# Gathering V apart from U in five of eight slots, with rows of weight zero left out

## The reference, cut to what matters

```
q = (xt @ w_query).reshape(TOKEN_BLOCK, PEER_HEADS, 2, PEER_HALF)
s = einsum('thpd,hpnd->thpn', q, sub_keys)
s_top, i_top = lax.top_k(s, 16)
...
best, pos = lax.top_k(cand, 16)          # 16 experts for each token and each of 8 heads
idx = take_along_axis(cand_idx, pos)
g = softmax(best)
u = expert_u[idx]
v = expert_v[idx]
act = gelu(einsum('td,thkd->thk', xt, u))
return einsum('thk,thkd->td', g * act, v)
```

## Time and profile before

| | us |
|---|---|
| median of 3 runs (1540.13 to 1544.98) | 1541.23 |
| the profiled execution's own time | 1543.3 |
| its span in the trace | 1541.5 |

### The profile page before, as it was taken

How to read it: one execution, slowest core, us unless ns; L and a number is a source line. 1 busy time by engine, 2 the same in 40 slices (tenths; PEclk the granted TensorE clock), 3 DMA queues, 4 the chain that set the end, 5 groups by cost and what they waited for, 6 DMA issues and landing times.

```text
span 1541.5 us, 24488 instructions
## 1 busy us (share of the span) xinstructions
PE 1415.1 (92%) x8308; PEld 1060.6 (69%) x8308; DVE 1099.3 (71%) x2390; ACT 785.9 (51%) x1804; POOL 342.2 (22%) x445
## 2 busy tenths in 40 slices
PE   9999999999999999999999899999877887777877
PEld 8898999998889999998989864444222332222222
DVE  6667877777768777577897687666666667666644
ACT  6656544456665444476964435444444444444433
POOL 1010011110110111111110134333333333333331
PEclk9999999999999999999999999999999999999999
DMA  9999899999999999999999499999999999999996
GB/s 356 355 337 334 281 399 398 388 392 340 353 325 331 403 389 403 386 362 337 344 329 352 149 388 414 422 421 421 421 422 421 421 420 422 422 421 421 417 422 266
DMA packets 119268, 578.23 MB, mean 375 GB/s; under 512 B 11472, under 2 KB 11616, under 8 KB 85904
## 3 DMA queue, kind: packets, MB, share of 16 engines
q0 software_dynamic: 79584, 432.01, 72.3%
q1 hardware_dynamic: 39168, 142.97, 24.6%
q10 hardware_dynamic: 432, 2.19, 0.4%
HBM read 576.08 MB, written 135.27 MB: 461 GB/s over the span
## 4 chain that ended last, share of the span: by engine, by line
PE 60%; DMA 23%; DVE 9%; ACT 5%; issue 3%; POOL 0%; POOLq 0%; DVEq 0%; ACTq 0%
DMA attn<-expert_uv,idx 15%; PE PS L655 8%; PE PS L651 8%; PE PS L646 8%; PE PS L1179 8%; PE PS L1143 7%; DMA ada<-w_ada 4%; DMA late<-expert_uv,idx 3%; PE PS L779 3%; PE PS L677 2%; PE PS L1106 2%; PE PS L889 2%; PE PS L893 2%; PE PS L894 2%; ACT wrg L1591 2%
## 5 line engine op out<-in xcount | busy, mean ns | idle before, releaser
L2360 DVE CUSTOM_DVE_ANT_0 late<-late,PS 128x1024 f32<-128x1024 f32 x128 | 156.2, 1220 | 112.9 <-DMA late<-expert_uv,idx 112.9
L1666 DVE TENSOR_TENSOR early_splits<-ring,early_splits 128x1024 fp32r<-128x1024 f32 x166 | 202.0, 1221 | 48.1 <-ACT early_splits L1245 47.9
L2360 DVE CUSTOM_DVE_ANT_0 attn<-attn,PS 128x1024 f32<-128x1024 f32 x128 | 156.1, 1220 | 96.7 <-DMA attn<-expert_uv,idx 95.0
L1245 ACT ACTIVATE early_splits<-ring 128x1024 fp32r<-128x1024 f32 x166 | 174.8, 1054 | 44.5 <-PE PS L646 35.7
L1583 ACT ACTIVATE gel<-dot 128x1 f32<-128x1 f32 x256 | 51.2, 200 | 266.9 <-DVE dot L2360 266.7
L1179 PE MATMUL PS<-late,wrg 128*128 128x512 f32 x288 | 145.3, 630 | 43.4 <-ACT wrg L1591 43.4
L593 POOL DMA_INDIRECT attn<-expert_uv,idx x128 | 120.9, 944 | 240.4 <-PE PS L1179 103.0
L1179 PE MATMUL PS<-attn,wrg 128*128 128x512 f32 x288 | 142.4, 619 | 31.8 <-ACT wrg L1591 31.6
L593 POOL DMA_INDIRECT late<-expert_uv,idx x128 | 119.9, 937 | 231.9 <-PE PS L1179 117.0
L1179 PEld LDWEIGHTS PS<-late,wrg 128*128 128x128 f32 x288 | 49.9, 191 | 135.4 <-ACT wrg L1591 98.1
L1179 PEld LDWEIGHTS PS<-attn,wrg 128*128 128x128 f32 x288 | 50.7, 193 | 123.5 <-ACT wrg L1591 82.3
(11 more groups left out here) (416 smaller groups left out, 3033.8 us busy)
## 6 DMA issues: line engine op xcount, KB each, us to landing
ring<-wstream SPq DMA_DIRECT2D x258, 512.0 KB, 9.1
expert_uv<-expert_u POOLq DMA_DIRECT2D x64, 1024.0 KB, 14.3
expert_uv<-expert_v POOLq DMA_DIRECT2D x64, 1024.0 KB, 15.8
ada<-w_ada POOLq DMA_DIRECT2D x32, 512.0 KB, 10.4
late<-w_ada POOLq DMA_DIRECT2D x16, 512.0 KB, 14.6
late<-wstream SPq DMA_DIRECT2D x4, 512.0 KB, 9.3
attn<-expert_uv,idx POOLq DMA_INDIRECT x128, 15.2
late<-expert_uv,idx POOLq DMA_INDIRECT x128, 15.2
```

The source lines that it names most:

```text
L1245: act.activation(hi_of(u), raw(u), ACT.Copy).then_inc(hi_ready, 1)
L1666: ve.tensor_tensor(lo_of(u), raw(u), hi_of(u).bitcast(F32), ALU.subtract).then_inc(units_begun, 1)
L2360: ve.tensor_tensor_reduce(row, row, H2N[n // 8], 1.0, 0.0, ALU.mult, ALU.add, dot[:, n % 2, k:k + 1]).then_inc(dot_ready, 1)
```

## The change

Slots 1, 4 and 7 (`JOINT`) stay as they were. In the other five slots POOL gathers only U from `expert_u` (4 KB a token), and V later, from `expert_v`, with a gather of its own, four rows later in POOL's list (`V_LAG`). Before that V gather DVE makes its indices (`pick_row`): the row's index where the weight is not zero, and that index plus 2^20 where the weight equals zero. The gather has a bound, and an index above it is passed over, so that nothing is copied for that token; what lay in the buffer stays and is multiplied by zero. U may be gathered again into a separate slot as soon as the dot of the row before in that slot is done (`dot_ready`); V waits for `row_used`. PE waits for `v_landed`, which is `row_landed` in the joint slots.

```diff
+JOINT = (1, 4, 7)
+V_LAG = 4
+NO_ROW = float(1 << 20)
...
+        idx_v = sb("idx_v", [P, SLOTS], U32)
+        no_row = sb("no_row", [P, SLOTS])
...
+        v_landed = [row_landed[k] if k in JOINT else sem(f"v_landed{k}") for k in range(SLOTS)]
+        tokens_marked, rows_picked = sem("tokens_marked"), sem("rows_picked")
...
+        def separate(rows):
+
+            return rows // SLOTS * (SLOTS - len(JOINT)) + sum(k not in JOINT for k in range(rows % SLOTS))
...
+                s = i % SLOTS
+                at = bass.IndirectOffsetOnAxis(ap=idx[:, n % 3, k:k + 1], axis=0)
+                if s in JOINT:
+                    if i >= SLOTS:
+                        gp.wait_ge(row_used, i - SLOTS + 1)
+                    gp.indirect_dma_start(UV[s], None, expert_uv, at).then_inc(row_landed[s], 16)
+                else:
+                    if i >= SLOTS:
+                        gp.wait_ge(dot_ready, i - SLOTS + 1)
+                    gp.indirect_dma_start(UV[s][:, 0:D], None, expert_u, at).then_inc(row_landed[s], 16)
+
+            def row_v(i):
+
+                s = i % SLOTS
+                if s in JOINT:
+                    return
+                gp.wait_ge(rows_picked, separate(i + 1))
                 if i >= SLOTS:
                     gp.wait_ge(row_used, i - SLOTS + 1)
-                gp.indirect_dma_start(UV[i % SLOTS], None, expert_uv,
-                                      bass.IndirectOffsetOnAxis(ap=idx[:, n % 3, k:k + 1], axis=0)
-                                      ).then_inc(row_landed[i % SLOTS], 16)
-
-            for i in range(ROWS):
-                row(i)
+                gp.indirect_dma_start(UV[s][:, D:2 * D], None, expert_v,
+                                      bass.IndirectOffsetOnAxis(ap=idx_v[:, s:s + 1], axis=0),
+                                      bounds_check=NKEYS * NKEYS - 1, oob_is_err=False).then_inc(v_landed[s], 16)
+
+            for i in range(ROWS + V_LAG):
+                if i < ROWS:
+                    row(i)
+                if i >= V_LAG:
+                    row_v(i - V_LAG)
...
             def weigh(i):
-                pe.wait_ge(row_landed[i % SLOTS], 16 * (i // SLOTS + 1))
+                pe.wait_ge(v_landed[i % SLOTS], 16 * (i // SLOTS + 1))
...
+            def pick_row(i):
+
+                n, k, s = i // EXPK, i % EXPK, i % SLOTS
+                if s in JOINT:
+                    return
+                ve.wait_ge(w_ready, i + 1)
+                ve.tensor_scalar(no_row[:, s:s + 1], wts[:, s:s + 1], 0.0, NO_ROW, ALU.is_equal,
+                                 ALU.mult).then_inc(tokens_marked, 1)
+                if i >= SLOTS:
+                    ve.wait_ge(v_landed[s], 16 * (i // SLOTS))
+                ve.wait_ge(tokens_marked, separate(i + 1))
+                ve.tensor_tensor(idx_v[:, s:s + 1], no_row[:, s:s + 1], idx[:, n % 3, k:k + 1],
+                                 ALU.add).then_inc(rows_picked, 1)
...
                     row_dot(n * EXPK + k)
+                    if n or k:
+                        pick_row(n * EXPK + k - 1)
```

More of the change, by code:

```diff
@@ L1175, in weigh_rows @@
                     for m in range(SLOTS):
-                        pe.wait_ge(row_landed[m], turn * 16 + 16 * (first // SLOTS + 1))
+                        pe.wait_ge(v_landed[m], turn * 16 + 16 * (first // SLOTS + 1))
                         pe.wait_ge(diag_ready, turn * SLOTS + (first + m + 1))
```

## The result

The changed kernel takes 1726.37 us (median of 4 runs, 1717.78 to 1731.4) against 1542.33 (4 runs) beside it: ratio 1.1184, interval 1.1156 to 1.1212. The forecast was 1574, range 1518 to 1620. The direction was right; the size was not, by 152 us. What follows reads the two profiled executions.

A forecast was written before the change was run, and what follows sets the result against it. The prediction took the DMA engines (99% busy, 420 to 422 GB/s) to bound the lookup. Its terms, +21 + 39 + 8 + 9 - 52 + 8 = +33 us on the median of 1541.2, gave 1574, range 1518 to 1620.

The forecast's parts named there:

- the dear gather: Rival: each bounded gather costs POOL 0.66 us more, 2.43 us a row, total 1623 us; chance 12%.
- the rival of zeros not skipped: Rival: zero-weight V rows are fetched in effect, steady rows at 2.49 or above, the gain goes, 1626 us; chance 8%.
- short flights: Rival: with engines running, a flight's fixed 3.0 us is smaller by 1.4, -24 over some 17 flights, 1550 us; chance 10%.
- -52: Gain in the steady rows: rows 72 to 127 16 us, rows 144 to 255 36 us, together -52.
- I take 2.20: Pace assumed for the steady rows, in us a row, between 2.13 by bytes and 2.27 by the loop.
- Half-size packets cost nothing by themselves: Bytes step: 4 KB packets keep 421 GB/s, as the weight stream in slices 1 to 23 was read to show.
- The loop that I did compute, 2.27 a row: Steady rows: dot, pick, V issue, 5.5 us flight and V bytes ahead close a four-row loop in 9.1 us.
- 52.0 a head: Early heads 3 to 7: loops of 14.3, 8.3 and 29.4 us make a head 52.0 us instead of 38.9.
- 39 + 8: Early rows' loss: three whole heads (row 18 to 66) +39 us, the last head up to its scores +8.
- PE's clock, +8 (bounds 0 and 24): PE idles 3 to 5 us some 15 times; half of them at 1.6 us are 12, some hidden, taken as +8.
- the start (+21: Rows before row 18: scores +12, ten rows to row 18 +5, ScalarE's table switches +4, together +21 us.
- head 8 (+9: Head 8's first block, rows 128 to 143: three loops of 8.1 us, 24 us for 6 rows instead of 15, +9.

The follow-up runs named there:

- Run 3: The changed kernel with ScalarE taking PE's results four rows behind (gates three) instead of one, scores behind k = 10 instead of 8: 1609.07 us, ratio 1.041.
- run 6: Control: the kernel before the change with only the late takes of Run 3: 1539.59 us, ratio 0.9988.
- run 2: The changed kernel with the marker at 0 instead of 2^20, so every V row is read while picks, waits and bound stay: 1771.11 us, ratio 1.1458.
- run 13: As 12, but V right behind U in POOL's list and indices made seven rows ahead: 1521.24 us, ratio 0.9854.
- 12: As Run 3, but V rows left out by their index, made ahead of the dot; computes another sum, so no candidate: 1566.52 us, ratio 1.0171.
- run 7: As Run 3, but with the pick behind the row's own dot instead of the next row's: 1592.57 us, ratio 1.0323.
- run 9: The kernel before with five of eight slots gathered as separate U and V, V right behind U, nothing skipped: 1570.88 us, ratio 1.0172.
- 11: As run 7, but a V row is left out when its dot is under -6, so no weight is waited for: 1571.02 us, ratio 1.0184.
- Run 14: As 12 (V four rows later, indices made ahead), but no V row left out: 1595.19 us, ratio 1.0345.
- run 1: The changed kernel with V gathered by the row's own unbounded index, no pick or wait for it, every row read: 1594.9 us, ratio 1.0318.

## Why the prediction was right or wrong

**Right: the sign and its place.** The heads where ScalarE takes queries and scores lose most, by the loop that the prediction drew: takes, weight, pick, V issue, V flight, PE. Run 3 takes it apart and run 6 shows that nothing else hangs on the takes. The waits stand where they were forecast: VectorE waits 58.0 us for a weight between 900 and 1060 us, where "some tens" were said; ScalarE's takes wait longer than forecast, 9 to 16 us each in rows 16 to 79, for 6 to 9. Bytes fell by 36.8 MB (432.0 to 395.2 in the software queue; 38 forecast), which is 44% of the separate V rows, in the bounds of 41 to 50. The bounded gather takes 0.997 us to issue, forecast 0.94, in its bounds; the dear gather falls, and so does the rival of zeros not skipped (run 2: 41 us). V's flight in the loop shown, from the start of its issue to PE's start, is 1073.04 - 1069.26 = 3.8 us and V(0)'s 4.2, forecast 4.1. The rule of 2.0 us and bytes over 436 (the Trainium skill, "DMA: Bandwidth & Descriptors", section "Anatomy of one DMA") gives an estimate of 2.7 and does not hold here; "short flights" falls with it.

**Wrong: the term "-52", the steady rows.** Of it -13 were for rows 80 to 127 and -36 for rows 144 to 255 (the rest, rows 72 to 79, is counted with the early rows here). They lost 9.9 and 19.1: +29 where -49 stood. "I take 2.20" was 2.69. This one step is 78 us of the 152. The runs split the late pace: 2.13 by bytes at 421 GB/s; 2.36 when nothing waits, since the rate of full engines falls to 379 (run 13); 2.54 with the lag (12); 2.69 with the wait for the weight (7). The step that failed first is to take 421 GB/s over to the new packets. "Half-size packets cost nothing by themselves" is off by little (414 GB/s in run 9); most of the fall comes once rows are left out. Nor could carry the sentence: slices 1 to 23 show at most 403 GB/s, not 420, and a weight stream is no gather with rows left out. The loop that I did compute, 2.27 a row, took the 5.5 us flight of a lone gather for a joint row; in runs 11 and 12 joint rows fly 7.5 and 7.6 us (medians between 1250 and 1490 us). But run 7, whose loop spans five rows, keeps 2.69, so this loop alone does not set the pace.

**Wrong: the length of the loops, "52.0 a head".** Measured between takes: 16 us for 14.3, 11.4 for 8.3, 34.7 to 37.4 for 29.4, some 64 in all. Three differences are seen: the pick's end to POOL's issue takes 0.79 us where I had counted none beyond the pick; PE's row and its scores run at the lower clock, 3.78 and 1.91; and if the eight rows between go at 2.7, as elsewhere, in place of 2.20, that is 4 us a head. Rows 16 to 79 cost +95 where +45 stood (39 + 8, less 2 for rows 72 to 79).

**Wrong: "PE's clock, +8 (bounds 0 and 24)".** The idle times were seen, but the price was put on half of 15 rows. Each head has three such loops, and the granted clock goes down and up between its two levels through all of them: 0.54 in the window of 1072 to 1076 us, in which the row shown takes 3.78 us, and 1.00 in that of 1064 to 1068. The means are 0.83 and 0.85 between 940 and 1060 us, and 0.97 and 0.94 there once the takes are late (run 3). How many of the 95 us are the clock's own is not separated by these runs; in the loop shown it is 1.9 + 0.9 of 11.4. A bound, as an estimate: a mean of 0.83 over the 255 us of rows 16 to 79 is some 87 us at the lower level, so the halved speed itself can have cost at most 44 us there.

**Too low: the start (+21, measured +32) and head 8 (+9, measured +25).** V(0) goes out 2.3 us later than forecast: row 0's weight is done 1.6 us later than in the trace before, and POOL's issue starts 0.80 us after the pick. The early query, which POOL's row 7 waits for, starts behind PE's slow row 0:

```profile
895.33 1.00 POOL L622 DMA_INDIRECT attn<-expert_v,idx_v  x1 [7.14 <-DVE idx_v L2406]
...
899.50 3.78 PE L1175 MATMUL PS<-attn,wrg 128*128 128x512 f32 x4 [4.40 <-DMA attn<-expert_v,idx_v]
...
903.07 4.64 PE L1151 MATMUL PS<-soft,late 128*128 128x258 f32 x16
...
907.98 0.94 POOL L608 DMA_INDIRECT late<-expert_uv,idx  x1 [7.86 <-PE PS L1151]
```

POOL stands for 7.9 us there, with V(3) and the gathers of rows 8 and 9 behind it, and row 7 goes out at 907.98, before at 898.95. That wait (`freed_by_query`) was in the code, and I did not follow POOL past it. Head 8's six takes follow one another with no free rows between, so their 4.09 a row is that of the early heads. And the end was in no term: from the last dot's start to the end it is 15.3 us now, 8.7 before, since the last V is gathered behind its dot.

On the traces the error is 188 - 33 = 155 us, and these terms add up to it: 78 for the steady rows, 50 for rows 16 to 79, 16 for head 8, 11 for the start, 8 ahead of the first dot and at the end, less the 8 for the clock, whose price the measured stretches hold already. The direction was not luck: the loops cost what they were said to, and more. But the forecast held a gain of 52 us that does not exist here.

**Which rival was nearest.** None. Those above the forecast, 1623 and 1626, had other mechanisms, and both fell. What was missing is a case in which the gain itself does not come: engines that are not full any more because V is late, and that move less when they are.

## What to carry to other kernels

Where a kernel is bound by full DMA queues, bytes saved count in full only if the queues stay full and the rate stays the same: price the rate of the new packets, and what the new order of issues makes later, before the bytes. A load whose index hangs on the newest result turns every stall of the engines that make the result into an idle queue; count all in-order waits in that circle, those of unrelated work (here taking a query out of PSUM) first. An experiment that gives nearly the same bytes without the dependence (runs 12 and 13) tells early whether the idea has room: here 24 us at best, and none with the lag.

## What the runs showed of the hardware

Between 1300 and 1500 us (for the change 1430 to 1630, so that head 8's loops are not in it) the single packets' records in the traces give, at full or nearly full engines:

| kernel | GB/s, share | 8 KB packets, mean (median) ns | 4 KB, mean (median) ns | 4 B packets |
|---|---|---|---|---|
| before | 421, 1.01 | 314 (312) | | 1279 |
| halves, all rows (9) | 414, 1.02 | 315 (314) | 163 (161) | 2045 |
| halves, all rows, lag 4 (14) | 404, 1.01 | 325 (309) | 163 (159) | 2001 |
| halves, rows left out (13) | 379, 0.99 | 347 (309) | 165 (159) | 5489 |
| the change | 336, 0.93 | 354 (309) | 180 (159) | 4578 |

```profile
1430.00:1630.00 200.00, 150.24 (x297) 59.37 (x295) 137.00 (x419) 81.36 (x242) 116.68 (x122) 0.91 0.93 336
```

- A 4 KB packet takes 163 ns, 6 more than half of 314. That is the small price of halves in the late rows (run 9).
- A row left out still has a packet, but a cheap one: 4 bytes in place of 4 KB, 9 ns by the mean. The software queue has 102624 packets in run 1 and in the change alike; every gather also has 16 packets of 4 bytes of its own (1279 for 80 gathers in the kernel before). The counts show it:

```profile
DMA packets 18005, 80.81 MB, mean 404 GB/s; under 512 B 2001, under 2 KB 2001, under 8 KB 14284
```

```profile
DMA packets 18423, 70.49 MB, mean 352 GB/s; under 512 B 5053, under 2 KB 5053, under 8 KB 14591
```

(Run 14, then 12.) The 3052 more of them at 9 ns are 0.9% of the engines' time in these 200 us.
- The 8 KB packets of the joint rows keep their median, but their mean is 325 and 333 ns with V four rows late and all rows read (runs 14 and 1) and 347 to 354 in the rows of the table where rows are left out: some take much longer. Of the fall from 414 to 379 GB/s (8.5%) between runs 9 and 13 this is 4.0 points (3998 x 32 ns of 16 x 200 us), the share, 1.02 to 0.99, is 3, and the 4-byte packets and slightly longer 4 KB packets are about one each. Why the 8 KB packets grow longer is open; it was not tried.
- A bounded gather of 128 indices is issued in 997 ns (median) whether rows are left out (the change) or not (run 2), an unbounded one in 937.
